# One state-space pass for blocks 0 and 1 of a two-branch encoder layer on one Trainium2 core

## The chip, the core and the metric

The kernel is one program on one core of a Trainium2 chip. A core has five engines with a queue of instructions each: TensorE (PE, matmuls into PSUM), VectorE (DVE), ScalarE (ACT), GpSimd (POOL) and SyncE (SP, which here only issues DMAs). They meet by semaphores alone. The metric is the device time of one execution in microseconds, as the median of several; less is better. The kernel before takes 2249.74 us (three runs, 2248.51 to 2253.14).

## The reference, cut to what matters

```python
h = rmsnorm(x, norm_mix);  z = h @ w_in                     # 1024 -> 1536
xl, gl, us = z[..., :512], z[..., 512:1024], z[..., 1024:]
xc = causal_conv(xl, width 4);  hl = rglru(xc)              # gates, then a scan over time
y_lru = hl * gelu(gl)
# state-space branch: 32 heads (groups) of 16 inputs and 64 complex states
x_t = lam_bar * x_{t-1} + B_bar u_t;   ys = Re(C x_t) + d * u_t
g = gelu(ys);  y_ssm = g * sigmoid(g @ w_glu + b_glu)
x = x + concat(rmsnorm(y_lru), rmsnorm(y_ssm)) @ w_out
h2 = rmsnorm(x);  x = x + (silu(h2 @ w_gate) * (h2 @ w_up)) @ w_down     # 1024 -> 2816 -> 1024
y = rmsnorm(x)
```

It runs on a prompt of 2048 tokens from a zero state and on a later chunk of 32 tokens from a given state. All is float32.

## The kernel before

The 2080 tokens are cut into five blocks of 416; the 32 later ones are the end of block 4. A block goes through a mixer (norm, input product, both branches, output product) and then a feed-forward stage. All engines walk through one list, `STEPS`, and each emits what it has to do for each step, so a step's place in the list is its place in every queue. `FIRST` is the list for the opening: the mixer of block 0, the tables of the state-space branch, and the input products of block 1. From there on the feed-forward stage of block b is a row of 55 places (gate, up and two halves of down), and `MIXER` (`SECOND` for block 1) says at which place of block b's stage each step of block b+1's mixer is emitted. So the mixers of blocks 1 to 4 lie inside a stage of large matmuls, and only block 0's stands alone.

Names of steps, which the prediction uses. `us`, `xl`, `gl` (4 each) are the twelve units of the input product; for blocks 0 and 1 a unit is 8 fp32 matmuls of 416 columns against a weight chunk straight from HBM (L1052), for the others three reduced-precision matmuls take the place of each (L960 to L962). `cv` is the convolution, `ga` the gates (L1063), `la` to `ld` the scan of the first branch, `glu` the gated product, `out` the output product, `n1`, `nl`, `ns`, `n2` the norms' sums, `h1`, `h2` the normalized rows.

The state-space branch works on groups of 8 tokens. Its columns are a block's 52 groups; `zst` stores `us` to HBM and `zl` loads it back with one (time in group, channel) per partition. Two heads make a pair, and there are 16 pairs. Step `s5 j` makes, for pair j, the inner products v (two matmuls, L1083) and, for pair j-2, the outputs y (four matmuls, L1073 and L1074). Between them stand on DVE the function `states` (three products from PSUM, a difference, a copy of the carried state, a scan over the columns L1334, two copies of halves) and on POOL a product, a difference and a copy of the last state (L688, L694, L699). The rotation tables of a pair (52+2 columns) are loaded by `load_t` from HBM, four buffers deep; `tb`, `ts`, `tr`, `tt` make and store them in the opening, in two parts of 8 heads. `gst` and `gld` bring the outputs back to channel order.

Weights go through a ring of six slots that SP fills in the order of use; ACT and DVE split each into two parts (L749 and L1157 on `w_hl`). In blocks 0 and 1 the input products use the weights unsplit. For block 0 the matmul is done on `rows0`, which carry only the norm's gain, and DVE multiplies by the root when it empties the bank (steps `ue`, `xe`, `ge`); for block 1 DVE makes the normalized rows `made1`, and ACT empties the banks.

Of the kernel before, what the change touches and what calls it, by code (L numbers as in the profile page):

```python
# [26 lines left out]
W5 = C5 + 2  # L27
NW, CS = 2 * W5, W5
# [5 lines left out]
GE = P // HG  # L34
D_FF = 2816
# [91 lines left out]

OWN = list(SPLIT)[:2 + EARLY]
assert [SRC[u] for u in OWN] == [("glu", 0, 0), ("glu", 0, 1)] + [("out", 0, j) for j in range(EARLY)]


def split_here(u):
    return u < NU and u in SPLIT and u not in OWN


def early(kind, b, j):
    return kind == "out" and b == 0 and j < EARLY

PREP = {}
for _k, _b, _j in STEPS:
    if _k in ("ck", "bt"):
        PREP[(_k, _j, 0)] = len(PREP)
        PREP[(_k, _j, 1)] = len(PREP)


USE = {}
for _k, _b, _j in STEPS:  # L150
    if early(_k, _b, _j):
# [6 lines left out]
    elif _k == "s5":  # L158
        if _j >= 2:
            USE[("y5", _b, _j - 2)] = len(USE)  # L160
# [1426 lines left out]
```

## Time and profile before

| | us |
|---|---|
| median of three runs | 2249.74 |
| profiled execution, first to last instruction | 2246.2 |
| TensorE busy (matmuls) | 2195.1 |
| VectorE busy | 1485.6 |
| ScalarE busy | 1069.3 |
| GpSimd busy | 363.3 |

The profiled execution's own time is its span, 2246.2 us, which counts from the first to the last instruction; the median of the runs is 3.5 us more, which lies around the span. Busy times are sums over the span, so they say nothing about a stretch; the windows in the rows below do. The opening reaches from 0 to 270.5 us, where the first gate product of block 0 starts.

### The profile page before, as it was taken

The page shows a single profiled execution, that of the slowest core. Times are in us where ns is not written, and L with a number is a line of the kernel's source. Part 1 is how long each engine was busy: PE and PEld are TensorE (multiplying, and loading weights), DVE is VectorE, ACT ScalarE, POOL GpSimd, SP SyncE. Part 2 cuts the span into 40 slices and gives each one's busy share as a digit, 9 for nine tenths or more (in the row PEclk, how much of TensorE's full clock was granted, in tenths as well). Part 3 has the DMA queues.
Part 4 walks back from the last instruction along what each step waited for, and adds up shares of the span by engine and source line. Part 5 has one row for each costly group of instructions (what it writes and reads, how often), then busy time and mean ns, then how long its engine had stood idle before and what let it go on. Part 6 is the DMA issues. An engine that isn't in the chain of part 4 may idle for free.

```text
span 2246.2 us, 30290 instructions
## 1 busy us (share of the span) xinstructions
PE 2195.1 (98%) x11590; PEld 2087.1 (93%) x11590; DVE 1485.6 (66%) x2540; ACT 1069.3 (48%) x1446; POOL 363.3 (16%) x438
## 2 busy tenths in 40 slices
PE   8898999999999999999999999999999999999997
PEld 4566899999999999999999999999999999999996
DVE  6857555787566667876665687676658875665444
ACT  4427423656544456464444565444455464432232
POOL 4022100232111002411110132202102411100001
PEclk9999999999999999999999999999999999999998
DMA  7964335464335365633355556335365643343331
GB/s 237 235 213 138 118 114 135 146 189 139 122 114 181 118 148 164 185 122 118 123 172 135 148 173 175 113 113 183 113 148 148 174 121 120 113 143 114 129 117 66
DMA packets 201759, 324.52 MB, mean 144 GB/s; under 512 B 89296, under 2 KB 132944, under 8 KB 201488
## 3 DMA queue, kind: packets, MB, share of 16 engines
q1 hardware_dynamic: 201488, 322.36, 47.5%
q8 instruction: 93, 1.52, 0.3%
q14 instruction: 50, 0.41, 0.1%
q0 software_dynamic: 128, 0.23, 0.0%
HBM read 298.09 MB, written 26.53 MB: 145 GB/s over the span
## 4 chain that ended last, share of the span: by engine, by line
PE 88%; DVE 6%; ACT 3%; issue 1%; POOL 1%; SPq 0%; DMA 0%; POOLq 0%; DVEq 0%; ACTq 0%
PE acc L960 26%; PE acc L962 26%; PE acc L961 25%; PE acc L1052 5%; PE acc L1083 1%; PE acc L1074 1%; PE acc L1063 1%; PE acc L1073 1%; DVE rstd L1273 1%; DVE x_acc L1157 1%; DVE w_hl L1157 1%; DVE act_hl L1157 1%; POOL tmp L659 1%; ACT act_hl L935 0%; SPq L542 0%
## 5 line engine op out<-in xcount | busy, mean ns | idle before, releaser
L960 PE MATMUL acc<-act_hl,w_hl 128*128 128x416 f32 x2448 | 866.6, 354 | 6.5 <-DVE act_hl L1157 4.9
L961 PE MATMUL acc<-act_hl,w_hl 128*128 128x416 f32 x2448 | 853.3, 349 | 0.0
L962 PE MATMUL acc<-act_hl,w_hl 128*128 128x416 f32 x2448 | 853.3, 349 | 0.0
L1157 DVE TENSOR_TENSOR w_hl<-w_raw,w_hl 128x1024 fp32r<-128x1024 f32 x416 | 514.9, 1252 | 63.2 <-ACT w_hl L749 61.7
L960 PEld LDWEIGHTS acc<-act_hl,w_hl 128*128 128x128 f32 x2448 | 460.0, 188 | 15.4 <-DVE act_hl L1157 7.6
L961 PEld LDWEIGHTS acc<-act_hl,w_hl 128*128 128x128 f32 x2448 | 460.7, 188 | 2.4 <-issue 1.9
L962 PEld LDWEIGHTS acc<-act_hl,w_hl 128*128 128x128 f32 x2448 | 459.9, 188 | 1.1
L749 ACT ACTIVATE w_hl<-w_raw 128x1024 fp32r<-128x1024 f32 x416 | 431.8, 1052 | 46.0 <-DMA w_raw<-in_w_ffn 45.6
L1157 DVE TENSOR_TENSOR x_acc<-x_acc,acc 128x416 f32<-128x416 f32 x480 | 265.8, 584 | 171.6 <-PE acc L962 167.3
L960 PE MATMUL acc<-ff_hl,w_hl 128*128 128x416 f32 x880 | 312.4, 355 | 4.8 <-issue 4.3
L659 POOL TENSOR_TENSOR tmp<-tmp 128x416 f32<-128x416 f32 x117 | 147.6, 1262 | 1009.7 <-ACT tmp L760 948.8
L961 PE MATMUL acc<-ff_hl,w_hl 128*128 128x416 f32 x880 | 307.4, 349 | 0.0
L962 PE MATMUL acc<-ff_hl,w_hl 128*128 128x416 f32 x880 | 307.2, 349 | 0.0
L1157 DVE TENSOR_TENSOR f_g<-f_g,acc 128x416 f32<-128x416 f32 x110 | 64.6, 587 | 318.6 <-PE acc L962 318.6
L688 POOL TENSOR_TENSOR s5p<-s5w,s5t 128x216 f32<-128x216 f32 x80 | 104.2, 1302 | 768.6 <-DVE s5w L1337 768.1
L953 ACT ACTIVATE f_g<-acc 128x416 f32<-128x416 f32 x110 | 56.9, 517 | 276.9 <-PE acc L962 276.6
L960 PEld LDWEIGHTS acc<-ff_hl,w_hl 128*128 128x128 f32 x880 | 165.7, 188 | 7.2 <-issue 5.9
L961 PEld LDWEIGHTS acc<-ff_hl,w_hl 128*128 128x128 f32 x880 | 165.9, 189 | 1.0 <-issue 0.8
L962 PEld LDWEIGHTS acc<-ff_hl,w_hl 128*128 128x128 f32 x880 | 165.7, 188 | 0.5
L760 ACT ACTIVATE tmp<-x_acc 128x416 f32<-128x416 f32 x104 | 55.2, 548 | 151.8 <-DVE x_acc L1157 103.0
L772 ACT ACTIVATE ff_hl<-f_g 128x416 fp32r<-128x416 f32 x110 | 59.9, 545 | 118.5 <-DVE f_g L1157 118.5
L1157 DVE TENSOR_TENSOR s5prod<-acc,s5t 64x104 f32<-64x104 f32 (+5 forms) x288 | 66.4, 244 | 46.0 <-issue 32.5
(197 smaller groups left out, 1925.8 us busy)
## 6 DMA issues: line engine op xcount, KB each, us to landing
w_raw<-in_w_ffn SPq DMA_DIRECT2D x330, 512.0 KB, 3.7
w_raw<-in_w_in SPq DMA_DIRECT2D x60, 512.0 KB, 3.3
s5y<-y_dram SPq DMA_DIRECT2D x80, 256.0 KB, 4.0
w_raw<-in_w_out SPq DMA_DIRECT2D x40, 512.0 KB, 3.3
s5t<-t_dram SPq DMA_DIRECT2D x64, 162.0 KB, 3.8
s5v<-v_dram SPq DMA_DIRECT2D x80, 128.0 KB, 3.9
x_acc<-in_x SPq DMA_DIRECT2D x4, 1664.0 KB, 8.1
out_y<-x_acc SPq DMA_DIRECT2D x8, 832.0 KB, 7.1
```

Source lines behind the costliest of these rows:

```text
L659: po.tensor_tensor(tmp[:, 2, 0:width(b)], tmp[:, 6 if m == 1 else 2, 0:width(b)], tmp[:, 6 + m % 2, 0:width(b)], ALU.add)\
L688: po.tensor_tensor(s5p[:, s, :, :, 0:w5], s5w[:, s, :, :, 0:w5], tab[:, 0:2, :, 0:w5], ALU.mult).then_inc(p_made, 1)
L749: act.activation(w_hl[u % RING][:, 0, :], w_raw[u % RING][:], ACT.Copy).then_inc(w_hi, 1)
L760: act.activation(tmp[:, 6 + k % 2, 0:width(b)], src, ACT.Square).then_inc(sq_done, 1)
L772: act.activation(ff_hl[:, c % 3, 0, 0:width(c // NF)], f_g[:, c % 2, 0:width(c // NF)], ACT.Copy).then_inc(ff_hi, 1)
L953: act.activation(f_g[:, c % 2, 0:tk], acc[:, GATE, 0:tk], ACT.Silu).then_inc(gate_free, 1)
L960: pe.matmul(out, w(0), x(0), start=first, stop=False)
L961: pe.matmul(out, w(0), x(1), start=False, stop=False)
L962: return pe.matmul(out, w(1), x(0), start=False, stop=last)
L1052: ins = pe.matmul(acc[:, bank, 0:tk], w_raw[UNIT[step] % RING][:, k * P:(k + 1) * P], rows(b)[:, k, 0:tk], start=k == 0, stop=k == KD - 1)
L1063: pe.matmul(acc[:, bank, 0:tk], w_gates[:, g, j, :], tmp[:, 4 + j % 2, 0:tk], start=True, stop=True)\
L1157: return v.tensor_tensor(out, x, y, op)
```

## The change

The blocks are grouped as (0, 1), (2), (3), (4), and the state-space branch runs once for each group. For the first group a head has 104 columns: v, the scan and y take both blocks at once, in `FIRST`, and `SECOND` has no `s5`, `zst`, `zl` or `gst` steps left. A PSUM bank takes 2 x 104 columns. The tables are 106 columns wide and are made in four parts of 4 heads instead of two of 8; the single groups load the first 54 columns of them. So that `us` of block 1 is there in time, its four units now stand ahead of the pass, and the other units of block 1 follow behind. Block 1 is treated as block 0 is: ACT multiplies its rows by the gain in place, DVE empties the banks with the root, and the rows are moved by one DMA (`mv`) to `made1` before the later units use them. The store and load of `us` go by quarters (`zst 0` to `3`, `zl 0` to `3`). Table buffers are three instead of four, and `s5prod`, `s5in` and `s5p` have one buffer instead of two.

```diff
+GROUPS = ((0, 1), (2,), (3,), (4,))
+GRP = {b: gi for gi, blocks in enumerate(GROUPS) for b in blocks}
+NG = len(GROUPS)
+W5 = max(map(len, GROUPS)) * C5 + 2
+CS, NW = W5, W5 + 1
...
-        s5t = [sb(f"s5t{i}", [P, 3, 2, W5]) for i in range(4)]
-        s5prod = sb("s5prod", [P, 2, 2, 2, C5])
...
+        T5, O5, A5, B5, X5 = [[take(n * W5 * 4) for _ in range(k)] for n, k in ((6, 3), (4, 1), (4, 2), (4, 1), (2, 2))]
+        s5t = {w: [at(f"s5t_{w}_{i}", [P, 3, 2, w], F32, o) for i, o in enumerate(T5)] for w in WIDTHS}
...
             def load_t(gt):
...
+                if gi == 0:
+                    sp.dma_start(dst[:], table[:, :, :, :, 0:w]).then_inc(t_in[gt % 3], 16)
+                    return
+                for h in range(2):
+                    to, of = slice(h * NP_, (h + 1) * NP_), table[h].rearrange("p n q c -> p (n q) c")
+                    for c0, c1, from_ in ((0, w, 0),) if gi < NG - 1 else ((0, k + 1, 0), (k + 1, w, k + 1)):
+                        sp.dma_start(dst[to].rearrange("p n q c -> p (n q) c")[:, :, c0:c1], of[:, :, c0 - from_:c1 - from_])                          .then_inc(t_in[gt % 3], 16)
...
+                elif kind == "mv":
+                    sp.wait_ge(h_made, 2 * KD)
...
+                    sp.dma_start(made1[:], rows1[:]).then_inc(moved, 16)
...
                 elif kind == "s5":
-                    gt = b * GP + j
-                    if j < GP and gt + 2 < NB * GP:
+                    gi = GRP[b]
+                    gt = gi * GP + j
+                    if j < GP and gt and gt + 1 < NG * GP:
                         if gt >= 2:
                             sp.wait_ge(p_done, gt - 1)
...
-                        load_t(gt + 2)
...
+                        load_t(gt + 1)
...
+                    elif (kind, b) == ("h1", 1):
+                        for k in H_PARTS[j]:
+                            act.wait_ge(sq_done, SQ_AT[("n1", 1)] + k + 1)
+                            act.activation(rows1[:, k, 0:tk], rows1[:, k, 0:tk], ACT.Copy, scale=v1(G_MIX + k)).then_inc(h_made, 1)
...
                         for q in range(2):
-                            ins = pe.matmul(acc[:, bank, q * cols5(b):(q + 1) * cols5(b)], s5v[gt % 3][:, q, :], u5(b)[:, 2 * j + q, :],
+                            ins = pe.matmul(acc[:, bank, q * n5:(q + 1) * n5], s5v[gt % 3][:, q, :], heads5(gi, j)[:, q, 0:n5],
                                             start=True, stop=True)
...
+                    elif b:
+                        tt(kept[:, j + (KL if kind == "xe" else 0), 0:tk], made, root, MUL).then_inc(m_freed(key), 1)
```

The step lists, a stretch of each word for word (the third number is the block where it is 1):

```diff
-('s5', 6), ('s5', 7), ('gst', 0), ('gg', 3), ('xl', 3), ('bx', 2), ('gld', 0), ('xe', 3), ('s5', 8), ('s5', 9), ('gl', 1, 1), ('s5', 10), ('s5', 11)
+('ge', 1, 1), ('gld', 0), ('la', 1), ('gl', 1, 1), ('lb', 1), ('wc', 0), ('s5', 8), ('s5', 9), ('gg', 0, 1), ('gst', 1), ('s5', 10), ('zl', 3), ('lc', 1), ('s5', 11)
```

Three places of the queues. First TensorE's in the opening, from the sum of squares of block 1 on to the first v of the pass. L1052 (L1095 after the change) is a unit of the input product, where `rows_80` and `rows_86` are block 0's or, in the second row after the change and behind, `rows_87` block 1's; L1011 and L1019 (L1052 and L1060) prepare the tables. Before:

```order
L1029 MATMUL acc<-tmp,ones 128x416 x8
L1011 MATMUL acc<-c1t_126,bb 16x128 x8
L1011 MATMUL acc<-c1t_127,bb 16x128 x8
L1019 MATMUL acc<-ident,bmt_128 128x128 x8
L1052 MATMUL acc<-rows_80,w_raw_63 128x416 x8
...
L1052 MATMUL acc<-rows_80,w_raw_66 128x416 x8
L1052 MATMUL acc<-made_84,w_raw_67 128x416 x8
L1083 MATMUL acc<-u_first,s5v_89 128x52 x2
```

And of the changed kernel:

```order
L1070 MATMUL acc<-tmp,ones 128x416 x8
L1095 MATMUL acc<-rows_87,w_raw_66 128x416 x8
L1052 MATMUL acc<-c1t_140,bb 16x128 x8
L1052 MATMUL acc<-c1t_141,bb 16x128 x8
L1095 MATMUL acc<-rows_87,w_raw_67 128x416 x8
L1095 MATMUL acc<-rows_87,w_raw_68 128x416 x8
L1095 MATMUL acc<-rows_87,w_raw_69 128x416 x8
...
L1095 MATMUL acc<-rows_86,w_raw_66 128x416 x8
L1128 MATMUL acc<-u_wide_79,s5v_95 128x104 x2
```

Four units of block 1 have come ahead of the first v, where one was; eleven units stand ahead of it before the change and thirteen after.

Second, TensorE's queue in the middle of the pass, around v of pairs 8 to 11. The rows with `s5y` are outputs of an earlier pair. Before:

```order
L1083 MATMUL acc<-u_first,s5v_91 128x52 x2
L1073 MATMUL acc<-u_first,s5y_93 128x52
L1074 MATMUL acc<-s5x,s5y_93 128x52
L1073 MATMUL acc<-u_first,s5y_93 128x52
L1074 MATMUL acc<-s5x,s5y_93 128x52
L1083 MATMUL acc<-u_first,s5v_89 128x52 x2
L1052 MATMUL acc<-made_84,w_raw_68 128x416 x8
```

And of the changed kernel, from v of pair 8:

```order
L1128 MATMUL acc<-u_wide_79,s5v_97 128x104 x2
L1118 MATMUL acc<-u_wide_80,s5y_99 128x104
...
L1128 MATMUL acc<-u_wide_79,s5v_95 128x104 x2
L1118 MATMUL acc<-u_wide_79,s5y_100 128x104
...
L1128 MATMUL acc<-u_wide_79,s5v_96 128x104 x2
L1118 MATMUL acc<-u_wide_79,s5y_98 128x104
...
L1128 MATMUL acc<-u_wide_79,s5v_97 128x104 x2
L1095 MATMUL acc<-made_90,w_raw_67 128x416 x8
```

Before, at most two pair steps follow one another without a unit between them; now pairs 8, 9, 10 and 11 do.

Third, VectorE's queue at the same place of the changed kernel, in front of and in pair 8: `kept` is the emptying of a bank of block 1, `w_hl` a weight split.

```order
L1202 TENSOR_TENSOR kept<-acc,rstd_57 128x416
L1205 SCALAR_TENSOR_TENSOR tmp<-tmp 128x416 x2
L1202 TENSOR_TENSOR w_hl_65<-w_raw_71,w_hl_65 128x1024
L1202 TENSOR_TENSOR s5prod_108<-acc,s5t_2_106 128x208
L1202 TENSOR_TENSOR s5prod_108<-acc,s5t_2_106 64x208 x2
L1202 TENSOR_TENSOR s5in_59<-s5prod_108 128x2x104
L1387 COPY s5in_59<-carry_54 128x2x2
L1392 SCALAR_TENSOR_TENSOR s5w_0_111<-s5t_2_106,s5in_59 128x212
L1394 COPY s5w_0_111<-s5w_0_111 64x212
L1395 COPY s5w_0_111<-s5w_0_111 64x212
```

Before the change the bank of that unit is emptied by ACT, and the rows of a pair have half the columns. Where the stage of block 0 had steps with L1083, L1073 and L1074 on TensorE, nothing stands now: 96 matmuls are gone there. Between the sum `n2` and the first gate product two units of block 1 stood, and now one.

## Rows read from the trace of the kernel before

**Rows 1.** The page: the span and busy time (us, share, instructions).
```profile
span 2246.2 us, 30290 instructions
PE 2195.1 (98%) x11590; PEld 2087.1 (93%) x11590; DVE 1485.6 (66%) x2540; ACT 1069.3 (48%) x1446; POOL 363.3 (16%) x438
```

**Rows 2.** Windows: stretch, length, busy (instructions) of each engine, granted clock, DMA share, GB/s.
```profile
core 0: us, PE busy (x) PEld busy (x) DVE busy (x) ACT busy (x) POOL busy (x), PEclk, DMA share, GB/s
19.48:110.56 91.08, 85.06 (x298) 48.40 (x296) 69.65 (x108) 36.06 (x57) 19.36 (x20) 0.96 0.82 222
110.56:192.83 82.27, 80.94 (x362) 53.62 (x360) 52.20 (x160) 31.36 (x51) 24.17 (x48) 1.00 0.63 202
192.83:270.52 77.69, 68.78 (x301) 56.59 (x301) 48.46 (x59) 42.31 (x57) 14.33 (x10) 0.98 0.36 113
270.52:690.00 419.48, 417.02 (x2279) 410.50 (x2278) 284.30 (x472) 208.76 (x276) 64.82 (x70) 1.00 0.45 136
```

**Rows 3.** Timeline of TensorE around one pair step (start, length, ...) in block 0's stage.
```profile
418.14 0.32 PE L1073 MATMUL acc<-u,s5y 128*128 128x52 f32 x2
...
418.96 0.61 PE L1083 MATMUL acc<-u,s5v 128*128 128x52 f32 x4
419.39 0.43 PE L960 MATMUL acc<-act_hl,w_hl 128*128 128x416 f32 x1
419.66 0.35 PE L961 MATMUL acc<-act_hl,w_hl 128*128 128x416 f32 x1
```

**Rows 4.** Waits of TensorE from 275 to 690 us: us in total, times, longest.
```profile
PE acc L1073 <- POOL carry L699: 1.3, 1, 1.3
```

**Rows 5.** Groups by form on TensorE: busy, mean ns of a record (two a matmul).
```profile
L1083 PE MATMUL acc<-u,s5v 128*128 128x52 f32 x256 | 38.5, 273 | 0.9 <-ACT u L905 0.8
...
L1011 PE MATMUL acc<-c1t,bb 128*16 128x128 f32 x64 | 7.5, 273 | 0.0
```

**Rows 6.** Timeline of TensorE in the opening, three places.
```profile
97.78 7.36 PE L1052 MATMUL acc<-rows,w_raw 128*128 128x416 f32 x16
...
207.41 0.71 PE L960 MATMUL acc<-act_hl,w_hl 128*128 128x416 f32 x1 [3.10 <-DVE act_hl L1157]
...
259.67 11.34 PE L1052 MATMUL acc<-made,w_raw 128*128 128x416 f32 x32
```

**Rows 7.** Timeline of VectorE: one pair of the state-space pass and the next's start.
```profile
111.21 0.82 DVE L1157 TENSOR_TENSOR s5prod<-acc,s5t 128x104 f32<-128x104 f32 x3 [4.37 <-PE acc L1083]
112.06 0.27 DVE L1157 TENSOR_TENSOR s5in<-s5prod 128x104 f32<-128x104 f32 x1
...
112.45 0.38 DVE L1334 TENSOR_TENSOR_SCAN s5w<-s5t,s5in 128x108 f32<-128x108 f32 x1
112.86 0.21 DVE L1336 COPY s5w<-s5w 64x108 f32<-64x108 f32 x1
...
113.33 0.82 DVE L1157 TENSOR_TENSOR s5prod<-acc,s5t 128x104 f32<-128x104 f32 x3
```

**Rows 8.** Timeline of GpSimd: the same pair, and a product beside a weight split.
```profile
113.38 0.64 POOL L688 TENSOR_TENSOR s5p<-s5w,s5t 128x216 f32<-128x216 f32 x1 [45.03 <-DVE s5w L1337]
114.10 0.42 POOL L694 TENSOR_TENSOR s5x<-s5p 128x108 f32<-128x108 f32 x1
114.58 0.19 POOL L699 COPY carry<-s5x 128x2 f32<-128x2 f32 x1
...
179.84 1.69 POOL L688 TENSOR_TENSOR s5p<-s5w,s5t 128x216 f32<-128x216 f32 x1 [0.92 <-DVE s5w L1337]
```

**Rows 9.** Groups on VectorE with 416 columns: from PSUM (page), a scan (420 to 1000 us).
```profile
L1157 DVE TENSOR_TENSOR x_acc<-x_acc,acc 128x416 f32<-128x416 f32 x480 | 265.8, 584 | 171.6 <-PE acc L962 167.3
...
L1298 DVE TENSOR_TENSOR_SCAN tmp<-tmp,lru_st 128x416 f32<-128x416 f32 x7 | 7.6, 1090 | 0.2
```

**Rows 10.** DMA issues: line, count, KB each, median us to landing.
```profile
s5t<-t_dram SPq DMA_DIRECT2D x64, 162.0 KB, 3.8
...
u_first<-z_first SPq DMA_DIRECT2D x8, 104.0 KB, 5.3
```

**Rows 11.** Timeline of VectorE: normalized rows of block 0, root to last pair.
```profile
260.51 2.75 DVE L1273 RECIPROCAL rstd<-rstd 128x416 f32<-128x416 f32 x1 [2.28 <-ACT rstd L765]
...
272.96 1.16 DVE L1157 TENSOR_TENSOR act_hl<-tmp,act_hl 128x416 fp32r<-128x416 f32 x2
```

More of the change, by code:

```diff
@@ L34 @@
 GE = P // HG
+GQ = GP // KL
 D_FF = 2816
@@ L137, in early @@
     return kind == "out" and b == 0 and j < EARLY
+MOVE = STEPS.index(("mv", 0, 0))
+LATE = [s for s in STEPS[MOVE:] if s[1] == 1 and raw(*s)]
+SOON = [s for s in STEPS[:MOVE] if s[1] == 1 and raw(*s)]
 PREP = {}
@@ L218, in build @@
         lru_st = sb("lru_st", [P, KL, 2])
+        rstd1 = sb("rstd1", [P, T])
+        WIDTHS = sorted({len(blocks) * C5 + 2 for blocks in GROUPS})
+        I5 = take(2 * W5 * 4)
+        s5in = {w: at(f"s5in_{w}", [P, 2, w], F32, I5) for w in WIDTHS}
         R0 = take(RING * 2 * U * 4)
@@ L236, in build @@
         U5 = top[0]
-        u5_all = sb("u5", [P, G, C5])
-        u5_first = at("u5_first", [P, G, C50], F32, U5)
+        u5_wide = [sb(f"u5_wide{i}", [P, GE, W5 - 2]) for i in range(2)]
+        u5_own = [at(f"u5_own{i}", [P, GE, C5], F32, U5 + 4 * i * GE * C5) for i in range(KL)]
         x_acc, act_hl = [], []
@@ new lines, in _ @@
+                    sp.dma_start(u5(gi, j)[:, :, 0:cols5(gi)], z_dram[gi][j].rearrange("g h s c -> (h s) g c"))\
+                      .then_inc(u_in[j], 16)
+                elif kind == "fv":
+                    sp.wait_ge(v_st[0], 16)
+                    load_v(j)
+                elif kind == "ft":
+                    for n in range(3):
+                        sp.wait_ge(t_st[n][0], 32)
+                    load_t(j)
+                elif kind == "fy":
+                    sp.wait_ge(c1_st[0], 16)
+                    sp.wait_ge(kt_st, 16 * L)
+                    for gt in range(3):
+                        load_y(gt)
@@ L1047, in _ @@
                     bank = m_bank(step)
+                    if step == LATE[0]:
+                        pe.wait_ge(moved, 16)
                     if b < 2:
@@ L1052, in _ @@
                             ins = pe.matmul(acc[:, bank, 0:tk], w_raw[UNIT[step] % RING][:, k * P:(k + 1) * P],
-                                            rows(b)[:, k, 0:tk], start=k == 0, stop=k == KD - 1)
+                                            rows(step)[:, k, 0:tk], start=k == 0, stop=k == KD - 1)
                         ins.then_inc(m_full, 1)
@@ L1259, in table, with columns @@
                 return tt(out[:, :, 0:kn], out[:, :, 0:kn], rt[:, :, 0:kn], op)
+            def columns(q, out):
+                g = slice(q * GE, (q + 1) * GE)
+                turned = rt[:, :, 0:8].rearrange("p g t h -> p g (t h)").rearrange("p g (h t) -> p g h t", h=HG)
+                for to, n, r in ((out[:], 0, 0), (turned, 1, 2)):
+                    ins = tt(to, bb[:, n, g, :].unsqueeze(3).broadcast_to([P, GE, HG, 8]),
+                             pw[:, r, g, 0:8].unsqueeze(2).broadcast_to([P, GE, HG, 8]), MUL)
+                link(ins)
+                return tt(out[:], out[:], turned, ADD)
             def weight_lo(u):
@@ L1376, in _ @@
                         v.wait_ge(c1_done, KL)
-                    table(j, 8, bmt[j % 2], bb[:, 0], 0, bb[:, 1], 2, 0, ADD).then_inc(bm_done, 1)
+                    columns(j, bmt[j % 2]).then_inc(bm_done, 1)
                 elif kind in ("n1", "nl", "ns", "n2", "nf"):
```

394 lines of the change are left out of this document (196 added, 198 removed).

## The prediction, made before the changed kernel ran

> **What bounds the kernel now.** I read the page first: TensorE is busy for 2195.1 of 2246.2 us [rows 1], so work taken from it shortens the kernel one for one, unless it was waiting there. Then the windows, cut where the opening's parts begin [rows 2]: the reader is to subtract TensorE's busy time from each length. In block 0's feed-forward stage (270.52 to 690) 2.5 us are idle in 419.5. In the opening it is 6.0 ahead of the state-space pass (19.48 to 110.56), 1.3 in the pass (110.56 to 192.83), 8.9 behind it (192.83 to 270.52). The change takes work out of the full stage, and in the opening it adds none but reorders it. So the question is how many of the saved microseconds come back as idle time of TensorE in the opening. Third, the timelines of VectorE and GpSimd for one pair give the chain v to carried state that TensorE has to wait for. Sums below are made against the profiled execution, 2246.2 us; the median of the runs is 3.5 us above it, and I add that at the end.
>
> **Removed from the stage.** Block 1's 96 matmuls of 52 columns. One pair step takes from 418.14 to 419.39, 1.25 us for six matmuls, 0.21 each, and the large matmul behind it takes 0.43 instead of 0.35 [rows 3]. 96 x 0.208 is 20.0; 18 steps x 0.08 is 1.4. One wait of an output product for GpSimd's copy goes with them, 1.3 us [rows 4]. Sum -22.7. DVE, POOL and ACT lose their pair work there too, which isn't on the path.
>
> **Wide matmuls.** The trace has no 104-column fp32 matmul. Records of 52 columns take 273 ns, and so do those of 128 columns [rows 5]; from the other side, a unit of 8 matmuls of 416 columns is 5.67 us [half of the last row of rows 6], 1.70 ns a column, which for 104 columns is 0.18 us, under the 0.21 that the narrow ones take. So the lower bound is 0 and I take 0; the upper one is doubling, 96 x 0.21 = +20, and it is a rival.
>
> **Ahead of the pass.** Thirteen units instead of eleven stand before the first v, so it moves from 110.56 by 2 x 5.67 to about 121.9. That is no cost: the units are missing later. The added work lies on others. ACT multiplies block 1's rows (8 instructions, earlier 8 on DVE); DVE empties 4 more banks; GpSimd makes the tables in four parts, twice the columns; SP issues four stores and loads of quarters and the 1.7 MB move. TensorE covers these with 5.67 us a unit, and GpSimd is busy for 19.4 of 91 us [rows 2]. The waits that stand there (tables' transposes behind DVE, gates behind the convolution) keep their place. I take 0; the bounds are -4 (most of the 6.0 covered by the added units) and +11 (the DMAs, below).
>
> **In the pass.** A pair on DVE is 2.12 us, 111.21 to 113.33 [rows 7]. With 416 columns a product from PSUM takes 584 ns against 273 with 104 (0.82 for three), 1.0 ns a column, and a scan 1090 ns against 380 with 108, 2.3 ns a column [rows 7, 9]. So the three products grow by 0.31, the difference by 0.10, the scan by 0.24, the two copies by at most 0.20: 3.0 us. GpSimd's three take 113.38 to 114.77, 1.39; from 108 to 216 columns it grows from 0.42 to 0.64, 2.0 ns a column, so 0.42 and 0.21 more: 2.0 us [rows 8]. From DVE's start to the carried state it is 3.56 now and 5.0 then. DVE as a whole has room: 52.2 us busy [rows 2], plus 16 x 0.85, plus nine banks that ACT emptied at 0.6 each, is 71 of about 87.
>
> The order is what costs. Pairs 8, 9, 10 and 11 follow one another on TensorE without a unit. In front of pair 8 DVE has a bank to empty (0.6), two products behind ACT's exponentials (1.2) and a weight split (about 1.2), so it starts pair 8 some 3 us after its v (estimate; 1.7 if ACT is never late). Output 8 is ready 5.0 later, 8 us after v, and only step 9 (1.3) covers it: 6.5 us idle. Output 9 is ready 3.0 behind it, covered by 1.3: 1.7 idle. Output 10 has a unit before it. Pairs 14 and 15 come together behind a scan on DVE: about 1.8. Sum +10; bounds 4 (DVE starts at once, the others hidden) and 17 (one more such place). Behind such a wait TensorE is slow: the unit at 97.78 takes 7.36 instead of 5.67 [rows 6], in a stretch whose clock is 0.96 [rows 2]. +1.7 for the long wait.
>
> GpSimd's durations are not constant. Its product takes 0.64 us beside DVE's PSUM products, but 1.69 beside a weight split [rows 8]. The Trainium skill, GPSIMD Engine Reference, section 1 (Specifications), says that it shares its SBUF interfaces with VectorE, with contention when that has two SBUF inputs; by that rule the trace agrees, and a fuller DVE stretches GpSimd's part of each link. In the run of four the wide product (1.06) lies beside the next pair's three products from PSUM (1.1), so I leave it out of the forecast, and it is a rival.
>
> **Behind the pass.** Between the pass and the gated product one unit stands in both kernels; 0, within 2 either way. Before the first gate product it is two units before and one after. Now the sum `n2` ends at 259.7, the units run 11.34 us to 271.0 [rows 6], and the last normalized rows come at 274.1 [rows 11], in time for a gate product of 24 matmuls (417.0 us for 2279 in block 0's stage, 0.18 each [rows 2]) that ends at 275.4. With one unit TensorE is free at 265.3, yet its last six matmuls can't start before 274.1 and end at 275.2. One unit less of work, the same end: +5.6 idle. The chain from the root at 260.5 to 274.1 isn't touched by the change.
>
> **Blocks 2 to 4.** Table loads are issued one step later with one buffer less, and read runs of 54 columns, 216 bytes, instead of a whole partition's 1296. The table's load lands in 3.8 us at 162 KB; a load of 104 KB in pieces of 208 bytes takes 5.3 [rows 10]. A load is issued two steps ahead of its use, and over two steps lies at least one place of the stage (24 matmuls, 4.4 us), so I expect under 1 us of DVE waiting in places, hidden by a ring two units ahead: +0.5, bounds 0 and +4. The Trainium skill, DMA: Bandwidth & Descriptors, section Specifications, wants 512 bytes or more for the line rate. By that rule these loads get slower, as the 5.3 does; if each of 48 pairs held TensorE for 0.1 us it would be +5, but in block 0's stage, with its pieces of 208 bytes in the loads of `us`, TensorE idles for 2.5 us in all, so it stays in the bounds.
>
> **Sum.** -22.7 + 0 + 10 + 1.7 + 5.6 + 0.5 = -4.9: a span of 2241.3, a median of 2244.8.
>
> **Rivals.** (B) The stalls aren't there: DVE starts each pair at once, and the run of four costs 1 us. For it: the pass now has 1.3 us of idle time though DVE interleaves the same scans. Against it: the chain is 1.4 us longer and the run twice as long. -22.7 + 5.6 + 0.5 + 1 = -15.6, 2234.1. (C) Slower: GpSimd's product and difference are stretched by 1.69/0.64, 2.6-fold, in the dense places, 4.6 us a pair instead of 2.0. Four links that TensorE waits for (8, 9, 14, 15) x 2.6 is +10.4, in sum +5.5, 2255.2. It decides from the point where one pair's GpSimd part is longer than DVE's 3.0. (D) DMAs hold the start of the pass: the tables' bytes double (16 x 162 KB, 2.6 MB) and the move adds 1.7 MB, 4.3 MB at the 222 GB/s of that stretch is 19 us, with engines 82% busy already; less the two units of cover 11.3, +8: sum +3, 2253. Against it: the move can go beside the last units and SP issues fewer loads of `u5`. (E) The wide matmuls cost by their columns: +20, sum +15, 2265. That the change doesn't do what it says is excluded by the queues: 96 matmuls are gone.
>
> **Chances.** Forecast 0.47, its own range -12 to +2; B 0.22, C 0.14, D 0.12, E 0.05. About 0.2%, 4.5 us, is what a measurement can tell from no change. Faster: 0.27 of the forecast, 0.21 of B, 0.02 of C, 0.50. Same: 0.16 + 0.01 + 0.07 + 0.03 = 0.27. Slower: 0.04 + 0.09 + 0.05 + 0.05 = 0.23. The range goes from just under B to just over C: 2232 to 2257.
>
> **What would show it.** The span from the first gate product of block 0 to that of block 1 shrinks by 22 to 24 us. The first v comes at about 122, the pass takes 87 us, the first gate product starts near 282 and is stretched by about 5 us, and the longest wait of TensorE in the pass stands before output 8, released by GpSimd's copy (L699). Records of 104 columns take 273 ns. Idle time before the first v above 12 us shows D, GpSimd's products above 2 us in the run C, an idle pass under 4 us B. The forecast is wrong if the opening loses less than 10 us or more than 25.

## The result, and the profile after

2320.39 us median (2319.15 to 2321.13) against 2249.68: ratio 1.0316, 95% interval [1.0303, 1.0328], 71 us slower, outside the range. The profiled execution is 71.1 us longer too. Its page, with the lines that answer to [rows 1], and the granted clock in 40 slices:

```profile
span 2317.3 us, 29682 instructions
PE 2203.5 (95%) x11398; PEld 2084.3 (90%) x11398; DVE 1477.4 (64%) x2416; ACT 1059.0 (46%) x1430; POOL 365.9 (16%) x407
...
PEclk9976699999999999999999999999999999999998
```

The 192 records are gone, yet TensorE is busy for 8 us more: in the third to fifth slice the clock falls. The windows are cut at the same events as [rows 2] (first product v, end of the pass, first gate product); the last is 418.7 us long, block 0's stage once more:

```profile
core 0: us, PE busy (x) PEld busy (x) DVE busy (x) ACT busy (x) POOL busy (x), PEclk, DMA share, GB/s
19.48:133.06 113.58, 95.66 (x335) 54.14 (x333) 74.43 (x102) 50.55 (x79) 45.36 (x38) 0.95 0.74 216
133.06:293.90 160.84, 108.57 (x358) 70.42 (x359) 80.22 (x177) 35.29 (x54) 41.61 (x50) 0.72 0.49 143
293.90:361.30 67.40, 59.65 (x273) 52.52 (x272) 36.99 (x46) 30.94 (x40) 10.38 (x8) 0.95 0.31 94
361.30:780.00 418.70, 415.90 (x2191) 408.95 (x2191) 268.57 (x372) 197.28 (x258) 28.14 (x22) 1.00 0.39 122
```

Ahead of the first v TensorE is idle for 17.9 us, more than the 12 that the prediction gave as the sign of its rival D. The pass takes 160.8 us where it took 82.3 and 87 was named. The first gate product starts at 361.3, 90.8 us later; from there to the end the kernel is 19.7 us shorter, so what was to be gained from there on (16.6 us by the forecast) is there. In the pass the DMA engines are busy for 0.49 and move 143 GB/s, less than the 0.63 and 202 of before. The waits of both engines say for what (us in total, times, longest; TensorE from 19 to 320, VectorE from 100 to 300):

```profile
PE acc L1118 <- POOL carry L733: 28.8, 5, 7.5
PE acc L1128 <- DMA u_wide<-z_dram: 16.9, 3, 14.2
...
DVE s5prod L1202 <- DMA s5t<-t_dram: 65.7, 14, 7.2
```

TensorE's own releaser is GpSimd's copy, as the prediction named it. One step further back, VectorE waits in 14 of 16 pairs for the table. TensorE's timeline shows the wait ahead of the first v and the three longest ahead of outputs:

```profile
133.06 1.18 PE L1128 MATMUL acc<-u_wide,s5v 128*128 128x104 f32 x4 [14.20 <-DMA u_wide<-z_dram]
...
218.91 0.76 PE L1118 MATMUL acc<-u_wide,s5y 128*128 128x104 f32 x2 [7.48 <-POOL carry L733]
...
228.99 0.75 PE L1118 MATMUL acc<-u_wide,s5y 128*128 128x104 f32 x2 [7.20 <-POOL carry L733]
...
286.07 0.76 PE L1118 MATMUL acc<-u_wide,s5y 128*128 128x104 f32 x2 [7.55 <-POOL carry L733]
```

The pass's DMAs (window 133 to 294; bytes; line, count, KB each, median us to landing), to be held against [rows 10]:

```profile
DMA packets 19030, 23.08 MB, mean 143 GB/s; under 512 B 10090, under 2 KB 13162, under 8 KB 18922
...
s5y<-y_dram SPq DMA_DIRECT2D x19, 256.0 KB, 12.5
s5t<-t_dram SPq DMA_DIRECT2D x14, 318.0 KB
s5v<-v_dram SPq DMA_DIRECT2D x16, 128.0 KB, 10.5
...
w_raw<-in_w_out SPq DMA_DIRECT2D x3, 512.0 KB, 11.1
```

Every load shown is late, not the tables' alone, on engines that are idle half the time. That fits some of the 16 engines being full and the others not. The changed `load_t` suggests a reason: its source is `t_dram[:, half * NP_:(half + 1) * NP_, n]`, whose first dimension is 2.

**Theory A.** Each wide table load goes over 2 of the 16 engines. By that, each of the two carries in the pass 14 x 163 KB of tables (the first two loads land ahead of it) and 1/16 of the other 18.5 MB, 3.44 MB in 160.8 us, 21.4 GB/s (an estimate from the rows above), and all other loads' shares on these two stand in their queues. The Trainium skill, DMA: Bandwidth & Descriptors, section Why a DMA increments its semaphore by 16 and not by 1, states such a rule: take in each of the two access patterns the slowest dimension whose size isn't 1; the DMA uses the largest number of engines, up to 16, that divides both sizes. By that rule it is 2 here and 16 in the kernel before; the runs below agree. **Rival R1:** twice the bytes with three buffers in place of four, loaded one step ahead. **Rival R2:** the pair's chain through GpSimd is what is late, and the table waits only cover it.

### The profile page after: what moved, and what is told of

It reads as the page before. It is cut to its first block, busy times and chain, and to the rows that moved or that the text cites. A ratio compares the mean times of both kernels' runs of the same rounds, so it can differ in the third digit from the quotient of the medians.

```text
span 2317.3 us, 29682 instructions
## 1 busy us (share of the span) xinstructions
PE 2203.5 (95%) x11398; PEld 2084.3 (90%) x11398; DVE 1477.4 (64%) x2416; ACT 1059.0 (46%) x1430; POOL 365.9 (16%) x407
## 4 chain that ended last, share of the span: by engine, by line
PE 85%; DVE 5%; DMA 4%; ACT 2%; SPq 1%; POOL 1%; issue 1%; POOLq 0%; DVEq 0%; ACTq 0%
PE acc L1001 26%; PE acc L1003 25%; PE acc L1002 25%; PE acc L1095 4%; DMA s5t<-t_dram 3%; DVE act_hl L1202 1%; PE acc L1106 1%; PE acc L1128 1%; DVE rstd L1328 1%; PE acc L1119 1%; POOL tmp L692 1%; PE acc L1118 1%; DVE x_acc L1202 1%; DVE w_hl L1202 1%; DMA u_wide<-z_dram 1%
## 5 line engine op out<-in xcount | busy, mean ns | idle before, releaser
L721 POOL TENSOR_TENSOR s5p<-s5w,s5t 128x216 f32<-128x216 f32 (+1 forms) x64 | 88.9, 1389 | 599.3 <-DVE s5w L1395 598.9
L1202 DVE TENSOR_TENSOR s5prod<-acc,s5t 64x104 f32<-64x104 f32 (+5 forms) x240 | 59.1, 262 | 99.6 <-DMA s5t<-t_dram 69.4
```

Of the source, the lines that this page charges most:

```text
L721: po.tensor_tensor(turned[:], made[:], tab[:, 0:2], ALU.mult).then_inc(p_made, 1)
L1202: return v.tensor_tensor(out, x, y, op)
```

## The experiments

Twelve kernels, each timed beside the kernel before. "Halves" stands for the first; "over 2 engines" is Theory A's name for a load whose source begins with a dimension of 2.

| kernel | median us | ratio to before [95%] |
|---|---|---|
| table loads in halves | 2255.19 | 1.0026 [1.0016, 1.0035] |
| before, loads over 2 engines | 2264.91 | 1.0065 [1.0050, 1.0080] |
| its control | 2249.30 | 1.0002 [0.9993, 1.0011] |
| before, three buffers | 2249.70 | 1.0001 [0.9991, 1.0010] |
| one DMA of 128 rows | 2255.48 | 1.0030 [1.0018, 1.0041] |
| pairs 8 to 15 over 2 engines | 2287.46 | 1.0169 [1.0152, 1.0186] |
| halves, unit in the run | 2255.60 | 1.0027 [1.0015, 1.0038] |
| halves, pairs first | 2258.47 | 1.0041 [1.0026, 1.0056] |
| halves, inputs first | 2250.12 | 1.0002 [0.9993, 1.0012] |
| that, order, four tables | 2251.26 | 1.0007 [0.9997, 1.0016] |
| inputs first, unit, early quarter | 2255.74 | 1.0033 [1.0022, 1.0044] |
| all edits | 2247.19 | 0.9991 [0.9982, 0.9999] |

**Table loads in halves.**

```diff
-                    sp.dma_start(dst[:], table[:, :, :, :, 0:w]).then_inc(t_in[gt % 3], 16)
+                    for h in range(2):
+                        sp.dma_start(dst[h * NP_:(h + 1) * NP_], table[h][:, :, :, 0:w]).then_inc(t_in[gt % 3], 16)
```

> The changed kernel, with each table load of the first pass issued as two DMAs of 64 partitions in place of one whose access pattern begins with a dimension of 2. Bytes, buffers, order and the step at which they are issued are unchanged. Theory A (one load goes over 2 of the 16 DMA engines, 318 KB of it, and all other loads queue behind on those two): the loads land in 4 to 7 us in place of 11 to 17, VectorE waits for tables under 10 us in place of 66, the wait of 14.2 before the first v goes to under 4 and the first v comes at 119 to 123, the pass has 5 to 15 us of idle TensorE, and the time is 2240 to 2256. Rival R1 (the bytes of the wide tables and three buffers in place of four, with the load one step ahead): nothing of that moves, table waits stay above 40 us and the time above 2295. Rival R2 (the pass is late for another reason, the pair's chain through GpSimd, and the table waits only cover it): table waits go, the waits for the carried state stay at about 29 us and the time is 2280 to 2320.

2255.19 us: 65 of the 71 us come back with nothing but the shape of 16 loads changed. By the windows it is 8 us ahead of the first v and 62 in the pass, less 4 behind it. The same DMA view of the pass (125 to 224):

```profile
DMA packets 18244, 22.00 MB, mean 222 GB/s; under 512 B 9642, under 2 KB 12714, under 8 KB 18126
...
s5y<-y_dram SPq DMA_DIRECT2D x19, 256.0 KB, 4.7
s5t<-t_dram SPq DMA_DIRECT2D x28, 159.0 KB, 4.6
s5v<-v_dram SPq DMA_DIRECT2D x16, 128.0 KB, 4.6
...
w_raw<-in_w_out SPq DMA_DIRECT2D x3, 512.0 KB, 3.6
```

Landing times of the other loads shown fall to between a third and a half, and VectorE's waits for tables from 65.7 us to 0.2. R1 and R2 fall. The first v at 125.03 was later than A said, and TensorE's idle time in the pass is 14.8 us, at the upper end.

**The fault put into the kernel before, its control, and three buffers there.** The DRAM tensor gets the halves as its first dimension, and block 0's loads (162 KB, four buffers, two steps ahead) become one DMA from it; the control loads in halves. The third has the old layout.

```diff
-        t_dram = nc.dram_tensor("t_dram", (P, GP, 3, 2, W5), F32).ap()
+        t_dram = nc.dram_tensor("t_dram", (2, P, GP, 3, 2, W5), F32).ap()
...
+                if gt < GP:
+                    sp.dma_start(dst[:], t_dram[:, 0:NP_, t]).then_inc(t_in[gt % 4], 16)
+                    return
```

```diff
-        s5t = [sb(f"s5t{i}", [P, 3, 2, W5]) for i in range(4)]
+        s5t = [sb(f"s5t{i}", [P, 3, 2, W5]) for i in range(3)]
...
-                    if j < GP and gt + 2 < NB * GP:
+                    if j < GP and gt and gt + 1 < NB * GP:
...
-                        load_t(gt + 2)
+                        load_t(gt + 1)
```

> The kernel before, with its tables' DRAM tensor laid out with the halves outermost, so that each of block 0's 16 table loads (162 KB) is one DMA whose access pattern begins with a dimension of 2. Four buffers and two steps ahead as before. Other blocks load in two DMAs of 64 partitions. Theory A: at 318 KB a load took 11 to 17 us in the changed kernel, so half the bytes over the same 2 engines are 6 to 9 us, 16 of them 96 to 140 us of two engines in a pass of 82 us: they hold the pass, and the other loads' shares on these engines come late too. Time 15 to 50 us above the control (e2_control). Rival R1 (bytes and buffers): the same bytes and buffers as before, so the same as the control within 3 us.

> Control: the kernel before with the same DRAM layout, all table loads in two DMAs of 64 partitions. Both theories: 2247 to 2253, table loads landing in 4 to 5 us; one more DMA issue on SyncE per step costs nothing.

> The kernel before with three table buffers in place of four and each table load issued one step ahead of its use in place of two, in all blocks. Theory A: loads over 16 engines land in about 4 us, steps in the opening's pass are 5 us apart on average, so 2248 to 2254. Rival R1 (buffers and lateness are what held the changed kernel): VectorE waits for tables in block 0's pass, 2270 or more.

The fault costs 15.6 us with half the bytes and all buffers, at the edge of what A said. The control and three buffers cost nothing: with three, VectorE does wait for tables for 8.2 us in block 0's pass (5 times, 2.9 the longest), and the time stays the same. VectorE's waits, and the bytes from 109 to 205 us, in the kernel with the fault:

```profile
DVE s5prod L1161 <- DMA s5t<-t_dram: 26.4, 8, 7.5
```

```profile
DMA packets 13042, 17.06 MB, mean 178 GB/s; under 512 B 4123, under 2 KB 9564, under 8 KB 13036
```

The 1849 table packets of 1296 bytes in these 96 us and 1/16 of the other 14.7 MB are 2.11 MB on each of the two: 22.0 GB/s, close to the changed kernel's 21.4. With half the bytes the two are still busy for the whole pass (estimates, by A's share).

**One DMA of 128 rows.** Whether the halves were faster for being two:

```diff
-                table = t_dram[:, half * NP_:(half + 1) * NP_, n]
+                table = t_dram[half, :, n]
...
-                            sp.dma_start(t_dram[to, :, t:t + GQ // 2, n], tq[j][src][:].rearrange("p (t q) c -> p t q c", q=2))\
+                            for half in range(2):
+                                sp.dma_start(t_dram[half, to * NP_:(to + 1) * NP_, t:t + GQ // 2, n],
...
```

> The changed kernel with the DRAM layout of the tables turned so that one pair's 128 rows follow one another, and the first pass's table load is again one DMA, but its access pattern begins with a dimension of 128. The tables are stored in 24 DMAs of 64 partitions in place of 12 of 128. Theory A (what counts is over how many engines the access pattern's first dimension lets a load go): as with the halves, 2251 to 2258. Rival (the halves were faster because they are two DMAs, in flight side by side): 2300 or more, loads landing in over 8 us.

2255.48, as the halves; loads of 318 KB land in 4.6 us. The first dimension counts, not the number of DMAs.

**Pairs 8 to 15 alone over two engines.**

```diff
+                if gi == 0 and t >= GP // 2:
+                    sp.dma_start(dst[:], table[:, :, :, :, 0:w]).then_inc(t_in[gt % 3], 16)
+                    return
...
```

> The table loads of pairs 0 to 7 in halves of 64 partitions (as in the kernel that took 2255.2 us), those of pairs 8 to 15 each as one DMA whose access pattern begins with a dimension of 2, as in the changed kernel. A test of the size by bytes: in the changed kernel's pass two engines would carry 16 x 163 KB of tables and 1/16 of the other 18.5 MB each, 3.76 MB in 160.8 us, 23.4 GB/s. Here the tables of eight pairs are 1.30 MB on each and the other loads of the pass's second half about 0.46 MB; 1.76 MB at 23.4 GB/s take 75 us where the halves take 43, so about 30 us more: 2275 to 2295, table waits of VectorE of 25 to 40 us, all from pair 8 on, and the first product at 125 as with the halves. Rival (what costs is the late first loads, the pass recovers): within 8 us of 2255.2. Rival (latency of single loads, hidden by the units): 2260 to 2268.

2287.46, where 75 us in place of 43 had given 2287; both rivals fall. That it met to 1 us is in part luck. The 23.4 GB/s counts 16 tables beside the 18.5 MB that are left when only 14 are taken out; at 21.4 the same 1.76 MB give 82 us and 2294, which is still in the range. The waits of VectorE are all in the second half of the pass, from pair 8 on:

```profile
DVE s5prod L1206 <- DMA s5t<-t_dram: 37.2, 8, 7.2
```

**The packets.** The traces keep each DMA packet with its start, duration and size, though not its engine. A wide table load is 128 packets of 2544 bytes, one a partition, and nothing else in these stretches has that size:

| table loads of the pass | a load's most packets in flight at once | us from its first packet to its last |
|---|---|---|
| changed kernel, all 16 | 3 or 4 | 6.6 to 9.0 |
| halves, all 16 (both halves of a load) | 12 to 20 | 1.5 to 3.3 |
| one DMA of 128 rows, all 16 | 13 to 19 | 1.2 to 2.9 |
| last kernel, pairs 0 to 7 (halves) | 13 to 19 | 1.4 to 4.0 |
| last kernel, pairs 8 to 15 (over 2 engines) | 3 or 4 | 6.6 to 8.8 |

So only the loads whose source begins with a dimension of 2 are confined to a few engines, and in the last kernel both kinds stand in one pass. In the changed kernel two packets are in flight most of the time. There a packet took 102 ns (median), 24.9 GB/s. In the changed kernel's pass the table packets took 200 us in sum, 100 on each of two engines; the other packets took 1048, 66 an engine if spread evenly. That fills two engines (166 of 160.8 us, since packets overlap a little) and leaves the others at 0.41 (an estimate).

That settles the large part. The rest is about the 10 us by which the halves miss the forecast. Their windows:

```profile
19.48:125.03 105.55, 99.30 (x334) 55.61 (x332) 74.56 (x101) 44.40 (x72) 46.96 (x38) 0.95 0.82 231
125.03:223.79 98.76, 83.97 (x345) 57.20 (x345) 78.31 (x176) 37.93 (x58) 41.96 (x50) 0.91 0.80 222
223.79:295.22 71.43, 63.68 (x286) 54.48 (x285) 40.04 (x47) 34.20 (x44) 10.38 (x8) 0.95 0.35 107
```

and the long waits of TensorE in the pass, before outputs 2, 8 and 13:

```profile
158.91 0.53 PE L1119 MATMUL acc<-u_wide,s5y 128*128 128x104 f32 x2 [2.27 <-DVE kept L1203]
...
187.92 0.76 PE L1119 MATMUL acc<-u_wide,s5y 128*128 128x104 f32 x2 [4.70 <-POOL carry L734]
...
213.34 0.47 PE L1119 MATMUL acc<-u_wide,s5y 128*128 128x104 f32 x2 [3.81 <-POOL carry L734]
```

**A unit in the run of four pairs.** The steps of one unit move; FIRST before and after, cut:

```diff
-('s5', 8), ('s5', 9), ('gg', 0, 1)
+('s5', 8), ('s5', 9), ('gl', 2, 1), ('ge', 2, 1), ('gg', 0, 1)
```

> The table loads in halves of 64 partitions (2255.2 us), and one unit (block 1's third gated projection, 5.7 us of TensorE) taken from behind the pass and put between pairs 9 and 10, so that the run of four pairs becomes two runs of two. The prediction's reason for its term of the dense run (output 8 comes 5 us behind the start of pair 8 and only one step covers it): the idle 4.7 us ahead of output 8 and the 2.7 us that the following 5.4 us lost at 0.6 of the clock go, so the pass gets 5.7 of work for nothing and is 97 to 100 us long with it; the wait for the gated output behind the pass (4.4 us) loses its cover and grows to about 10. Time within 3 us of 2255.2, more likely 1 to 2 below. Rival (the stall is VectorE's backlog, not the missing cover): the wait moves to output 10 or 9 with 3 to 5 us, and the time is 2258 to 2261.

2255.60, the same as the halves, as expected. The wait before output 8 is gone, but a new one stands before v 12, for a load that the rival did not name:

```profile
201.15 1.18 PE L1129 MATMUL acc<-u_wide,s5v 128*128 128x104 f32 x4 [4.40 <-DMA u_wide<-z_dram]
```

The last quarter of the inputs is issued on SyncE behind step 10, which now stands behind the unit.

**Pairs first on VectorE.**

```diff
-('la', 1), ('gl', 1, 1), ('lb', 1), ('wc', 0), ('s5', 8), ('s5', 9)
+('gl', 1, 1), ('s5', 8), ('s5', 9), ('la', 1), ('lb', 1), ('wc', 0)
...
-('ld', 3), ('s5', 13), ('xl', 2, 1), ('wc', 1), ('xe', 2, 1), ('s5', 14), ('s5', 15)
+('s5', 13), ('ld', 3), ('xl', 2, 1), ('xe', 2, 1), ('s5', 14), ('s5', 15), ('wc', 1)
```

> The table loads in halves (2255.2 us), and in the order of work, two products and a weight split moved from ahead of pair 8 to behind pair 9, and the LRU's last scan and a weight split from ahead of pairs 13 and 14 to behind pairs 13 and 15. TensorE's order is the same. The prediction's reason (the run of pairs waits for what VectorE has ahead of a pair): VectorE starts pair 8 within 0.3 us of its product in place of 1.5, the wait before output 8 falls from 4.7 to about 3.3 us, that before output 13 from 3.8 to under 1, and GpSimd's product of pair 13, 2.12 us beside a weight split, to about 1.1; with the slow stretch behind them gone 4 to 7 us less, 2248 to 2251. Rival (the waits are set by GpSimd's part and the loads of tables, not by VectorE's order): within 2 us of 2255.2.

2258.47, against both. VectorE starts pair 8 at once and the wait before output 8 is 3.78, near the 3.3 said; but it then comes to pair 13 before the table:

```profile
207.68 1.15 DVE L1203 TENSOR_TENSOR s5prod<-acc,s5t 128x208 f32<-128x208 f32 x3 [2.47 <-DMA s5t<-t_dram]
```

and the wait before output 13 is 5.85, where under 1 was expected. The chain of the halves shows it already, from GpSimd's pair 11 over the table load of pair 13 (three buffers, one step ahead) to its product:

```profile
200.01 0.44 POOL carry L734
...
200.93 6.22 DMA s5t<-t_dram
...
210.10 2.12 POOL s5p L722
```

**Inputs loaded first.**

```diff
-('fv', 0), ('ft', 0), ('fv', 1), ('ft', 1), ('fv', 2), ('zl', 0), ('zl', 1)
+('zl', 0), ('zl', 1), ('fv', 0), ('ft', 0), ('fv', 1), ('ft', 1), ('fv', 2)
```

> The table loads in halves (2255.2 us), and on SyncE the loads of the first two quarters of the heads' inputs issued ahead of the first loads of v matrices and tables, which wait for the stores of the v matrices to land (7.1 us, to 116.7). Theory: the 2.5 us before the first v are this load's place in the queue; it lands before 119, the first v starts at 121 to 123 in place of 125.0, the unit behind it runs at full clock, 2 to 4 us less: 2251 to 2253. Rival (the v matrices' and tables' loads are then the last to land): the first v stays at 124 to 126 and the time within 1.5 us of 2255.2.

2250.12, 5 us less where 2 to 4 were expected; the first v is at 122.3, near the prediction's 121.9, and the unit behind it takes 5.77 us in place of 6.96.

**Together.** All three empty block 1's first gated rows ahead of the last convolution. The first adds the fourth table buffer (in `f_g`), loads two steps ahead and VectorE's order; the second the unit and the last quarter early, with three buffers; the third all of it.

```diff
+        s5t4 = [s5t[W5][i] for i in range(3)] + [at("s5t4", [P, 3, 2, W5], F32, F0)]
...
-                        load_t(gt + 1)
+                        load_t(ahead)
```

```diff
-('gst', 1), ('s5', 10), ('zl', 3)
+('gst', 1), ('zl', 3), ('s5', 10)
```

> The kernel with halves and the inputs loaded first (2250.1 us), plus the edit of VectorE's order that alone cost 3 us, plus a fourth table buffer in the first pass (in the memory of the gate product's rows, which are idle until then) with each table load issued two steps ahead, plus block 1's first gated rows evacuated ahead of the last convolution. Theory (the edit of the order failed because VectorE then came to pairs 9 and 13 before their tables: waits of 1.1 and 2.5 us that the one step ahead made): table waits are under 0.5 us in all, the waits before outputs 8 and 9 sum to under 4, before output 13 under 2.5, and the time is 2243 to 2248. Rival (GpSimd's part of a pair is stretched beside the moved work, tables or not): waits for the carried state stay above 9 us and the time at 2250 to 2254.

> Halves, inputs loaded first (2250.1 us), block 1's first gated rows evacuated ahead of the last convolution, the unit in the run of four pairs, and the load of the last quarter of the inputs issued ahead of step 10, since TensorE waited 4.4 us for it when only the unit was moved. Three table buffers. Theory (each term of the pass is a wait with its own releaser, and the run of four pairs costs what the prediction gave it): no wait over 1 us before pairs 8 to 12, the wait of 4.4 gone with the slow stretch behind it, the pass with its tenth unit 94 to 98 us long, the gated output's waits behind it at 7 (they were 4.4 with the cover): 2241 to 2247. Rival (another wait takes the place): 2248 to 2252.

> Both of the two kernels before this one together: four table buffers, VectorE's order, the unit in the run, the inputs' last quarter early. If the pass's waits are separate, 2238 to 2244; if VectorE is full by then (78 of 99 us busy in the pass) and its order only shifts waits, no better than the kernel with the unit and three buffers, within 2 us of it.

2251.26 and 2255.74: neither adds to inputs first, and the second loses 5.6 us, more than its rival allowed. The first fell to its rival: VectorE waits for no table there, yet the waits for the carried state are 9.6 us, 5.7 before outputs 8 and 9 and still 3.85 before output 13. In the second VectorE waits 7.6 us for a table:

```profile
DVE s5prod L1203 <- DMA s5t<-t_dram: 9.2, 3, 7.6
```

At most 2 us of that are the early quarter's: SyncE ends the stores of `gst` at 187.55 and issues the table load at 189.56, behind the quarter. With the unit moved alone the same wait is already 5.2. With two steps ahead all table waits are 1.5, and all edits give 2247.19, 2.4 us under before, the one version of the twelve whose interval lies below 1, if barely. It is above the 2238 to 2244 expected. Its pass has a tenth unit, the clock is nearly full, and TensorE is busy for 83.9 of 94.6 us:

```profile
122.87:217.50 94.63, 83.92 (x354) 54.09 (x355) 78.28 (x176) 39.11 (x59) 40.56 (x50) 0.98 0.89 248
```

Behind the pass the gated output, its cover moved, has two waits of 3.79 and 3.91 us where one of 4.45 stood.

## Why the prediction was wrong

**The step that failed** is the price of the first pass's table loads. The sum has nothing for them, neither ahead of the pass nor in it. The bound of +11 and rival D (+8) took the 4.3 MB at the 222 GB/s of all engines and looked at them ahead of the pass alone. "Blocks 2 to 4" weighed the shape of the later blocks' loads (pieces of 216 bytes), but not that of the first pass's. The only landing time it names is that of [rows 10], where the source begins with 128 partitions; the new source begins with 2. As priced, D gave 2253; the same bytes over two engines gave 2320. The price is 65 us, by the halves, and 62 of it lie in the pass; it was in no bound. The Trainium skill, DMA: Bandwidth & Descriptors, names the case in its section Rules for kernel authors: an outermost dimension of fewer than 16 confines a DMA to at most that many engines.

The other steps are read from the halves. The forecast's pass is its sum here, 82.3 - 5.7 + 10 + 1.7 (its text gave 87 among the signs):

| term | forecast | halves |
|---|---|---|
| first gate product to the end | -22.7 + 5.6 + 0.5 = -16.6 | -19.5 |
| first v, later than 110.56 | +11.3 | +14.5 |
| pass | 88.3 | 98.8 |
| behind the pass | 72.0 | 71.4 |

- **Stage, right.** It lost what the 96 matmuls take. The stretched first gate product costs 2.7 us (three waits of 0.85 to 0.93), not 5.6: the normalized rows come at even distances of 2.3 us, and the waits lie between them. With -22.7 and +2.7 that leaves 0.5 for blocks 2 to 4, as forecast. Their loads of 81 KB in pieces of 216 bytes land in 3.9 us in the halves; in the control, in pieces of 1296 bytes, they land in 3.8. So the slowing that the prediction drew from the 512 bytes hardly shows in the landing. In the changed kernel VectorE waits 3.7 us for tables outside the opening.
- **Wide matmuls, right.** Where the clock is nearly full (all edits), records of 104 columns take 275 to 279 ns against 273 [rows 5]. Rival E falls.
- **Ahead of the pass, 3.1 us too small.** The idle time is 6.3 us, as before's 6.0. TensorE's busy time is 99.3, where 85.1 and two units make 96.4: the rest is busy time at the lower clock (0.80 over the last unit ahead of the first v).
- **A pair, right.** On VectorE 2.88 us (3.0 forecast). From the product's start to the carried state it took 5.6 before output 8, 5.0 forecast: GpSimd's part was 2.6, not 2.0, stretched beside the next pair, so something like rival C's mechanism is there at a quarter of its size. Its sign, products above 2 us in the run, didn't come (1.08 for pairs 8 to 10, 1.48 for 11); pair 13's took 2.12 beside a weight split. That the halves' 2255.2 is C's figure too is chance. VectorE's and GpSimd's rows of pair 8, which answer to [rows 7, 8]:

```profile
182.31 1.14 DVE L1203 TENSOR_TENSOR s5prod<-acc,s5t 128x208 f32<-128x208 f32 x3
```

```profile
185.24 1.08 POOL L722 TENSOR_TENSOR s5p<-s5w,s5t 128x424 f32<-128x424 f32 x1 [5.43 <-DVE s5w L1396]
186.39 0.83 POOL L729 TENSOR_TENSOR s5x<-s5p 128x212 f32<-128x212 f32 x1
187.29 0.58 POOL L734 COPY carry<-s5x 128x2 f32<-128x2 f32 x1
```

- **Waits in the pass, right in place, 3.5 us too small.** 14.8 of idle time, 1.3 of it there before, against 10. Output 8 waits for 4.7 with L734 as its releaser (6.5 forecast). Not seen: 2.3 us before output 2, where a bank's emptying stands on VectorE behind a convolution; 2.2 ahead of the first unit on the moved rows, for which the profile names no releaser; and 3.8 before output 13. The chain of that last one goes over a table load with one step ahead, but it stays at 3.85 where no table is waited for, so VectorE's and GpSimd's other work in front of pair 13 is enough for it.
- **Clock, far too small.** 1.7 us was priced for one wait. TensorE's busy time is 84.0 where one unit less than 80.94 is 75.3: 8.7 us, at a granted clock of 0.91. Five of six waits of over 2 us here and ahead of the pass were followed by a slow stretch: the unit behind the 2.5 us before the first v takes 6.96 in place of 5.77 us, and steps 10 and 11 behind the 4.7 take 5.4, at a granted clock of 0.50, where 2.7 is usual. The sixth, the 2.2, was followed by full clock here and by a unit of 7.5 us at 0.77 in two other kernels (one DMA of 128 rows, inputs first), so the same wait doesn't cost the same each time.

With the halves in it, the changed kernel takes 2255.2: within the range, but 10 above the forecast, and slower than before. So the forecast of a gain was wrong apart from the table loads too, by 3 us ahead of the pass and 10.5 in it, less 3.5 behind (spans: 2251.4 against 2241.3).

Open: that the lower clock follows from the waits is read from the order of rows; no run changed it alone. Which engines carry a confined load isn't recorded. That they are two rests on the packets in flight, the bytes, the lengths and the rule.

## What to carry to other kernels

When a change touches a DMA, read both its access patterns from the left: bytes that go over 2 engines in place of 16 load each of these eight times as much and hold every other load's part behind them. The sign in this profile was that all loads landed late (12.5 us in place of 4.7) while the DMA share fell (0.49 against the halves' 0.80). And a forecast of several waits needs the slow stretches behind them, two thirds of the waits here (8.7 us for 13.5), and each moved step's place in the queue that issues the loads.

## What the runs showed of the hardware

Loads whose source began with a dimension of 2 had at most 4 packets in flight, those that began with 64 or 128 up to 20. Over whole passes two engines moved an estimated 21.4 GB/s each with table rows of 2544 bytes (changed kernel), and 22.0 with rows of 1296 (before, loads over 2 engines); a single packet of 2544 bytes ran at 24.9. Their lateness reached back into the issuing queue: in the changed kernel one 128 KB load took SyncE 6.22 us to issue, in the halves at the same place 0.9:

```profile
114.94 6.22 SPq L504 DMA_DIRECT2D s5v<-v_dram  x1
```
